# The end of a decoder trunk: the last expert weights requested before the wait for the scatters, the weighting of results behind the last pair's low parts, and all four token sums on TensorE

## The chip, the cores and the metric

The kernel runs on one core of one Trainium2 chip. The metric is the device time of one execution in microseconds, lower is better; the median of three runs before the change is 745.61 us.

Four engines appear below: TensorE (PE, matmuls; PEld are its weight loads), VectorE (DVE), ScalarE (ACT) and GpSimd (POOL). SyncE (SP) issues most DMA transfers from its own instruction queue (SPq). Each engine runs its own instructions in program order; semaphores order work between engines.

## The reference

One layer of `x + mixers(norm(x))`, then `x + moe(norm(x))`, then a final RMSNorm, for 512 tokens of width 1024 in float32. The change sits in the last two steps:

```
t = xn.reshape(b * s, d)                      # 512 x 1024
# each token picks one group of 8 experts, and 2 experts in it; combine holds their two weights
for e in range(32):
    hid = silu(t @ w_expert_gate[e]) * (t @ w_expert_up[e])      # width 256
    out = out + combine[:, e:e + 1] * (hid @ w_expert_down[e])
x = x + out
return rms_norm(x, final_norm_g)
```

## The kernel before, in words

The mixers come first and are not touched. The MoE then runs in 17 turns: 16 pairs of experts, and one turn between them for tokens that overflow an expert. An expert has 64 slots for tokens, so a pair fills the 128 partitions. In each turn TensorE multiplies the gathered tokens by the pair's gate and up weights (L1911, 64 matmuls), transposes the next pair's tokens (L1884), transposes the hidden rows (L1929), and multiplies by the down weights in two column halves `b` (L1950, 8 matmuls each); `y_ps` counts these halves. ScalarE and VectorE move the two halves out of PSUM into `ye`, and GpSimd scatters the rows to `y_dram` in HBM. The weights, 1 MB for each of the three matrices of an expert, arrive in a ring of 20 slots (`raw_slots`, named `ring_z`, `ring_x`, `ring_y`, `ring_w`, `ring_h`, `ring_p`, `ring_e`), requested by SyncE in order of use; `wait_reuse` (L477 ff.) holds each request until its slot is free.

The last two pairs (`KEPT`, turns 15 and 16) are not scattered. Their outputs are weighted on chip and split in a high part `yeh` (ScalarE, L976) and a low part `yel` (VectorE, the `stt` helper L1013), 128x512 for each half. `kept_products(k, t)` (L1868) adds them to the token sums of tile `t` by a one-hot matrix `pick`: two halves, each a `yeh` and a `yel` matmul of 512 columns. `k` is 0 for turn 15 and 1 for turn 16. All other results are read back from `y_dram` into four token tiles `yt[0]` to `yt[3]` (buffers `ring_z`, `ring_x`, `ring_x`, `ring_y`), two requests of 512 KB per tile, both counted by one semaphore. `gather_results` (VectorE) then forms x2 + w0 y0 + w1 y1 per tile in two operations on 128x1024; `comb_in` counts them.

The end, which the change touches:

- SyncE (L543 to L552) waits for the last two scatters, requests the results, and only then the two down matrices of the last pair, as four half-matrices: the first column halves with `d_half`, then the second ones.
- VectorE in the last turn weights tile 0 ahead of `hid`, tiles 1 and 2 ahead of the first low part, tile 3 between the low parts.
- The PSUM sums `TOTALS` are two banks per tile. Down products go to banks 5 and 6, the transposed hidden rows to bank 4. TensorE adds the weighted results of tiles 0 and 1 into their sums by `add_sum` (L1876), two float32 matmuls with the identity; tiles 2 and 3 are added by VectorE instead (`added`, L1533), two operations of 128x512 each. TensorE finishes the tiles in the order 3, 0, 2, 1, and they are normed and stored in the order 0, 3, 1, 2.
- For each tile ScalarE squares and sums a row (L1003) and takes the root (L1005); VectorE takes the reciprocal (L1524) and scales by it and `final_norm_g` (`scaled`, one 128x1024 `stt`); SyncE stores it (L570).
- Before the norms, every engine reads `flag`, a number in SBUF, and branches on it. With these inputs the branch is not taken.

## Times and profile before

| | us |
|---|---|
| three runs | 744.25, 745.61, 746.86 |
| median | 745.61 |
| span of the profiled execution, first to last instruction | 742.8 |
| median less span | 2.8 |
| PE, PEld, DVE, ACT, POOL busy | 696.6, 512.4, 342.6, 245.7, 90.3 |

The profile gives one execution by its span alone; the 2.8 us between it and the median stand for what lies around the span (the runs themselves lie 2.61 us apart). The trace gives each instruction its start and duration in us from the span's start, and behind it, in brackets, how long its engine was idle before it and what ended that. A row can merge several instructions (x8). In the rows, a matmul's duration contains the drain of its pipeline, so consecutive matmuls overlap.

### The profile page before, as it was taken

How to read it: one execution, taken by the hardware profiler on the slowest of the kernel's cores; microseconds unless marked ns; L12 is line 12 of the kernel's file. 1: busy time of each engine (PE TensorE's matmuls, PEld its weight loads, DVE VectorE, ACT ScalarE, POOL GpSimd, SP SyncE). 2: the span in 40 equal slices, each digit the busy share in tenths (PEclk: the TensorE clock that was granted, in tenths of full speed). 3: DMA queues.
4: the chain of work that ended last, by engine and by line, in shares of the span. 5: the costliest groups of instructions: out<-in, count | busy, mean ns of one | idle time of the engine just before them, and what ended most of it. 6: DMA issues, size and time to landing. Idle time of an engine off the chain costs nothing.

```text
span 742.8 us, 9617 instructions
## 1 busy us (share of the span) xinstructions
PE 696.6 (94%) x3863; PEld 512.4 (69%) x3863; DVE 342.6 (46%) x635; ACT 245.7 (33%) x397; POOL 90.3 (12%) x135
## 2 busy tenths in 40 slices
PE   5999999999999999999999999699999999978785
PEld 4888988877777777688888888566555564645443
DVE  5378994255556666555446215614211112112156
ACT  7232135465656666454243211200111111001014
POOL 2001912001010100200002000202111111211000
PEclk9999999999999999999999999789999999999998
DMA  6523234332221112392405699489999999999982
GB/s 230 170 67 105 93 87 142 128 127 72 71 67 41 59 48 70 104 336 71 138 5 226 277 367 345 164 324 394 415 420 421 419 422 420 417 421 418 423 330 116
DMA packets 61582, 166.58 MB, mean 224 GB/s; under 512 B 8084, under 2 KB 39905, under 8 KB 49116
## 3 DMA queue, kind: packets, MB, share of 16 engines
q1 hardware_dynamic: 55900, 153.86, 54.0%
q0 software_dynamic: 5632, 12.05, 4.3%
q8 instruction: 32, 0.52, 0.3%
q14 instruction: 18, 0.15, 0.1%
HBM read 158.31 MB, written 15.99 MB: 235 GB/s over the span
## 4 chain that ended last, share of the span: by engine, by line
PE 83%; DMA 8%; DVE 3%; ACT 2%; SPq 2%; issue 1%; POOL 0%; POOLq 0%; ACTq 0%; DVEq 0%
PE psum L1552 30%; PE psum L1911 12%; PE psum L1648 12%; PE psum L1950 7%; PE psum L1823 6%; DMA ring_y<-in_w_expert_up 4%; PE psum L1660 3%; DMA ring_e<-in_w_expert_down 2%; PE psum L1700 2%; PE psum L1727 1%; DMA y_dram<-ye,slots 1%; PE psum L1673 1%; PE psum L1929 1%; PE psum L1716 1%; SPq L552 1%
## 5 line engine op out<-in xcount | busy, mean ns | idle before, releaser
L1552 PE MATMUL psum<-xh,wh 128*128 128x512 f32 x256 | 99.9, 390 | 1.5 <-DVE xl L1013 1.5
L1552 PE MATMUL psum<-xh,wl 128*128 128x512 f32 x256 | 99.7, 389 | 0.0
L1552 PE MATMUL psum<-xl,wh 128*128 128x512 f32 x256 | 99.6, 389 | 0.0
L1016 DVE TENSOR_TENSOR wl<-raw,wh 128x1280 fp32r<-128x1280 f32 (+4 forms) x37 | 71.8, 1946 | 40.8 <-ACT wh L761 21.2
L1013 DVE SCALAR_TENSOR_TENSOR hid<-psum,rslot,act_g 128x256 f32<-128x256 f32 x17 | 8.2, 484 | 119.8 <-ACT act_g L967 119.8
L967 ACT ACTIVATE act_g<-psum,rslot 128x256 f32<-128x256 f32 x17 | 8.0, 473 | 155.4 <-PE psum L1911 155.4
L1552 PEld LDWEIGHTS psum<-xh,wh 128*128 128x128 f32 x256 | 48.1, 188 | 11.5 <-DVE xl L1013 1.7
L1552 PEld LDWEIGHTS psum<-xh,wl 128*128 128x128 f32 x256 | 48.1, 188 | 10.1
L1552 PEld LDWEIGHTS psum<-xl,wh 128*128 128x128 f32 x256 | 48.1, 188 | 9.9
L1648 PE MATMUL psum<-xh,wh 128*128 128x512 f32 x128 | 53.1, 415 | 0.0
L1648 PE MATMUL psum<-xh,wl 128*128 128x512 f32 x128 | 50.2, 392 | 0.0
L1648 PE MATMUL psum<-xl,wh 128*128 128x512 f32 x128 | 50.0, 390 | 0.0
L1013 DVE SCALAR_TENSOR_TENSOR sg<-cu,ch,sg 128x512 f32<-128x512 f32 x60 | 48.8, 884 | 0.0
L1911 PE MATMUL psum<-ring_w,xT 128*64 128x256 f32 x224 | 40.2, 394 | 4.9 <-DMA ring_h<-in_w_expert_up 4.9
L1911 PE MATMUL psum<-ring_h,xT 128*64 128x256 f32 x224 | 38.8, 384 | 1.3 <-DMA ring_e<-in_w_expert_up 1.3
L1468 DVE COPY ye<-psum 128x512 f32<-128x512 f32 x15 | 10.4, 692 | 59.4 <-PE psum L1950 59.4
L667 POOL DMA_INDIRECT y_dram<-ye,slots x15 | 15.2, 1010 | 172.8 <-DVE ye L1468 160.2
L1911 PE MATMUL psum<-ring_e,xT 128*64 128x256 f32 x208 | 34.8, 394 | 0.0
L1911 PEld LDWEIGHTS psum<-ring_w,xT 128*64 128x64 f32 x224 | 23.3, 142 | 12.7 <-issue 7.2
L1911 PEld LDWEIGHTS psum<-ring_h,xT 128*64 128x64 f32 x224 | 23.0, 139 | 11.7 <-issue 3.9
L1222 DVE TENSOR_TENSOR gp<-gs,psum 128x512 f32<-128x512 f32 x16 | 11.0, 687 | 39.2 <-PE psum L1552 38.4
L894 ACT ACTIVATE gs<-psum,bg 128x512 f32<-128x512 f32 x16 | 10.9, 687 | 52.6 <-PE psum L1552 52.6
(329 smaller groups left out, 1495.2 us busy)
## 6 DMA issues: line engine op xcount, KB each, us to landing
raw<-in_w_gate SPq DMA_DIRECT2D x16, 1024.0 KB, 6.2
raw<-in_w_in SPq DMA_DIRECT2D x9, 1024.0 KB, 5.8
ring_w<-in_w_expert_gate SPq DMA_DIRECT2D x7, 1024.0 KB, 22.9
ring_w<-in_w_expert_up SPq DMA_DIRECT2D x7, 1024.0 KB, 21.8
ring_h<-in_w_expert_gate SPq DMA_DIRECT2D x7, 1024.0 KB, 22.7
ring_h<-in_w_expert_up SPq DMA_DIRECT2D x7, 1024.0 KB, 24.6
ring_e<-in_w_expert_up SPq DMA_DIRECT2D x7, 1024.0 KB, 28.9
ring_h<-in_w_expert_down SPq DMA_DIRECT2D x6, 1024.0 KB, 25.1
```

The costliest lines, as they stand in the source:

```text
L667: pool.indirect_dma_start(out=y_dram[:, :], out_offset=bass.IndirectOffsetOnAxis(ap=slots[n, p], axis=0), in_=ye[n, s, :], in_offset=None, ...
L894: act.activation(gs[:, m, :], gate_bank(cg, m)[:, :], ACT.Sigmoid, bias=bg[:, d:d + 1]).then_inc(S["gate_mul"], 1)
L1013: return dve.scalar_tensor_tensor(out=out_, in0=a, scalar=s, in1=b, op0=o0, op1=o1)
L1016: return dve.tensor_tensor(dst, src, hi.bitcast(F32), ALU.subtract)
L1222: dve.tensor_tensor(gp[:, m, :], gs[:, m, :], branch_bank(cg, m)[:, :], ALU.mult).then_inc(S["gate_free"], 1)
L1552: last = nc.tensor.matmul(dst, a, b, start=start and n == 0, stop=stop and n == len(seq) - 1)
L1648: last = nc.tensor.matmul(bank[6 + n % 2][:, :], a[:, c, f], b[:, c, :], start=c == 0 and q == 0, stop=c == KC - 1 and q == 2)
L1660: last = nc.tensor.matmul(bank[5][:, :], a[:, j, f], b[g][:, j, :], start=j == 0 and q == 0, stop=j == BJ - 1 and q == 2)
L1700: nc.tensor.matmul(bank[0][:, q0:], k_s[r:r + HD, j, kt * P:(kt + 1) * P], q_s[r:r + HD, j, q0:], start=True, stop=True).then_inc(S["z_psu ...
L1823: last = nc.tensor.matmul(bank[t][:, :], x_[:, t, c, :], w_[:, b, c, :], start=c == 0 and m == 0, stop=c == KC - 1 and m == 2)
L1911: last = nc.tensor.matmul(bank[2][half, m * FE:(m + 1) * FE], xT[:, k, half], w[h][:, k, :], start=k == 0 and m == 0, stop=k == KC - 1, sk ...
L1950: last = nc.tensor.matmul(bank[5 + b][half, :], hidT[:, m, half], w_d[h][:, m, b * T:(b + 1) * T], start=m == 0, stop=m == FE // P - 1)
```

## The change

Order of requests on SyncE: the last pair's two down matrices are requested whole, like all others, ahead of the wait for the scatters; the four half-matrix requests behind the results are gone, and with them the semaphore `d_half`. TensorE waits once, for both whole matrices.

VectorE: nothing of the results is weighted ahead of `hid`. Tile 0 is weighted ahead of both low parts, tiles 1 to 3 behind them.

Sums: `TOTALS[t]` is now banks 2t and 2t+1 for every tile; down products go to banks 4 and 5, the transposed hidden rows to bank 6. TensorE adds the weighted results of all four tiles; VectorE's `added` is gone. Tiles are finished, normed and stored in the order 0, 1, 2, 3.

```diff
-        TOTALS = [psum[:, 0:2, :], psum[:, 2:4, :], psum[:, 5:7, :], psum[:, 4:8:3, :]]
-        ADDED = NT // 2
-        SUMMED, NORMED = (3, 0, 2, 1), (0, 3, 1, 2)
+        TOTALS = [psum[:, 2 * t:2 * t + 2, :] for t in range(NT)]
...
-            last_down = [unit_no(0, LAST, half, 2) for half in range(2)]
-            for w in range(NU, last_down[0]):
+            for w in range(NU, len(units_of(0))):
...
             for s in range(2):
                 sp_e.wait_ge(scattered[s], 16 * (NPAIR // 2 - s))
             load_results()
-            for w in last_down:
-                wait_reuse(0, w)
-            for b in range(2):
-                for w in last_down:
-                    slot = ring_at(0, w)[0]
-                    i, kind, e = units_of(0)[w]
-                    cols = slice(b * T, (b + 1) * T)
-                    sp_e.dma_start(raw_slots[slot].rearrange("p (m n) -> p m n", m=FE // P)[:, :, cols],
-                                   ed_v[e].rearrange("p (m n) -> p m n", m=FE // P)[:, :, cols]).then_inc(ring_full[slot] if b else S["d_half"], 16)
...
-            for n, t in enumerate(NORMED):
-                sp_e.wait_ge(S["fin_last"], n + 1)
+            for t in range(NT):
+                sp_e.wait_ge(S["fin_last"], t + 1)
...
-            for n, t in enumerate(NORMED):
-                if t < ADDED:
-                    act.wait_ge(S["c_ps"], SUMMED.index(t) + 1)
-                    total = TOTALS[t]
-                else:
-                    act.wait_ge(S["comb"], NT - t)
-                    total = halves(yt[t][:, 0, :])
-                act.activation(halves(yt[t][:, 1, :]), total, ACT.Square, accum_out=stat[:, 0, t:t + 1]).then_inc(S["sq_done"], 1)
+            for t in range(NT):
+                act.wait_ge(S["c_ps"], t + 1)
+                act.activation(halves(yt[t][:, 1, :]), TOTALS[t], ACT.Square, accum_out=stat[:, 0, t:t + 1]).then_inc(S["sq_done"], 1)
...
-                    if isinstance(c, int) and i == LAST:
-                        gather_results(1, range(1))
                     dve.wait_ge(S["silu"], E + 1)
...
+                        if k:
+                            gather_results(1, range(1))
                         for b in range(2):
-                            if k:
-                                gather_results(1, range(1 + 2 * b, 3 + b))
                             half = slice(b * T, (b + 1) * T)
                             dve.wait_ge(S["y_hi"], 2 * k + b + 1)
-                            stt(yel[:, 1 - k, half], bank[5 + b][:, :], w_kept[:, k:k + 1], yeh[:, 1 - k, half].bitcast(F32),
+                            stt(yel[:, 1 - k, half], bank[4 + b][:, :], w_kept[:, k:k + 1], yeh[:, 1 - k, half].bitcast(F32),
                                 ALU.mult, ALU.subtract).then_inc(S["y_lo"], 1)
                         dve.sem_inc(S["y_b"], 1)
+                        if k:
+                            gather_results(1, range(1, NT))
...
             dve.wait_ge(S["gfin_in"], 16)
-            def scaled(t):
-
-                dve.wait_ge(S["root"], NT + 2 + NORMED.index(t))
+            for t in range(NT):
+                dve.wait_ge(S["root"], NT + 2 + t)
                 st.link(dve.reciprocal(stat[:, 2, t:t + 1], stat[:, 1, t:t + 1]))
-                total = TOTALS[t] if t < ADDED else halves(yt[t][:, 0, :])
-                stt(halves(yt[t][:, 0, :]), total, stat[:, 2, t:t + 1], halves(gfin[:, :]), ALU.mult, ALU.mult).then_inc(S["fin_last"], 1)
-
-            def added(t):
-
-                dve.wait_ge(S["c_ps"], SUMMED.index(t) + 1)
-                for b in range(2):
-                    half = slice(b * T, (b + 1) * T)
-                    ins = dve.tensor_tensor(yt[t][:, 0, half], yt[t][:, 0, half], TOTALS[t][:, b, :], ALU.add)
-                ins.then_inc(S["comb"], 1)
-
-            added(3)
-            scaled(0)
-            scaled(3)
-            added(2)
-            scaled(1)
-            scaled(2)
+                stt(halves(yt[t][:, 0, :]), TOTALS[t], stat[:, 2, t:t + 1], halves(gfin[:, :]), ALU.mult, ALU.mult).then_inc(S["fin_last"], 1)
...
             add_sum(0, 0, False)
-            for t in SUMMED:
-                if t == 1:
-                    add_sum(t, 0, False)
-                if t == 2:
-                    kept_products(0, t, True, False)
-                kept_products(1, t, False, True).then_inc(S["c_ps"], 1)
+            kept_products(1, 0, False, True).then_inc(S["c_ps"], 1)
+            kept_products(0, 2, True, False)
+            for t in range(1, NT):
+                kept_products(1, t, False, False)
+            for t in range(1, NT):
+                add_sum(t, 0, False).then_inc(S["c_ps"], 1)
```

SyncE's queue, from the last gate and up matrices to the results, before:

```order
L457 DMA ring_p1<-in_w_expert_gate 128x2048 [waits gu_done]
L457 DMA ring_e0<-in_w_expert_up 128x2048 [waits gu_done]
L540 DMA ring_z<-y_dram 128x1024 [waits sc1,sc0]
L540 DMA ring_z<-y_dram 128x1024
L540 DMA ring_x<-y_dram 128x1024 x4
L540 DMA ring_y<-y_dram 128x1024 x2
L552 DMA ring_e0<-in_w_expert_down 128x2x512 [waits gu_done]
```

and after the change (`sc0`, `sc1` are the scatters' semaphores):

```order
L455 DMA ring_p1<-in_w_expert_gate 128x2048 [waits gu_done]
L455 DMA ring_e0<-in_w_expert_up 128x2048 [waits gu_done]
L455 DMA ring_e0<-in_w_expert_down 128x2048 [waits gu_done]
L455 DMA ring_e1<-in_w_expert_down 128x2048 [waits gu_done]
L537 DMA ring_z<-y_dram 128x1024 [waits sc1,sc0]
L537 DMA ring_z<-y_dram 128x1024
L537 DMA ring_x<-y_dram 128x1024 x4
```

The down matrices moved from behind the eight requests for results to ahead of them, and ahead of the wait that these carry.

VectorE's last turn (`hid` is the hidden product, the `ring_` rows the weighting of results, `yel` the low parts), before:

```order
L1013 SCALAR_TENSOR_TENSOR ring_z<-ring_z,cw 128x1024 [waits comb_in]
L1013 SCALAR_TENSOR_TENSOR hid<-psum,rslot,act_g 128x256 [waits silu,comb_in]
L1013 SCALAR_TENSOR_TENSOR ring_x<-ring_x,cw,x2 128x1024 [waits x1]
L1013 SCALAR_TENSOR_TENSOR ring_x<-ring_x,cw 128x1024 [waits comb_in]
L1013 SCALAR_TENSOR_TENSOR ring_x<-ring_x,cw,x2 128x1024 [waits x2s,comb_in]
L1013 SCALAR_TENSOR_TENSOR ring_x<-ring_x,cw 128x1024 [waits comb_in]
L1013 SCALAR_TENSOR_TENSOR yel<-psum,w_kept,yeh 128x512 [waits y_hi,comb_in]
L1013 SCALAR_TENSOR_TENSOR ring_y<-ring_y,cw,x2 128x1024 [waits x3]
L1013 SCALAR_TENSOR_TENSOR ring_y<-ring_y,cw 128x1024 [waits comb_in]
L1013 SCALAR_TENSOR_TENSOR yel<-psum,w_kept,yeh 128x512 [waits y_hi,comb_in]
L1474 TENSOR_LOAD flag [waits flag_ready]
```

and after the change:

```order
L996 SCALAR_TENSOR_TENSOR hid<-psum,rslot,act_g 128x256 [waits silu]
L996 SCALAR_TENSOR_TENSOR ring_z<-ring_z,cw,x2 128x1024 [waits x0]
L996 SCALAR_TENSOR_TENSOR ring_z<-ring_z,cw 128x1024 [waits comb_in]
L996 SCALAR_TENSOR_TENSOR yel<-psum,w_kept,yeh 128x512 [waits y_hi,comb_in]
L996 SCALAR_TENSOR_TENSOR yel<-psum,w_kept,yeh 128x512 [waits y_hi]
L996 SCALAR_TENSOR_TENSOR ring_x<-ring_x,cw,x2 128x1024 [waits x1]
L996 SCALAR_TENSOR_TENSOR ring_x<-ring_x,cw 128x1024 [waits comb_in]
L996 SCALAR_TENSOR_TENSOR ring_x<-ring_x,cw,x2 128x1024 [waits x2s,comb_in]
L996 SCALAR_TENSOR_TENSOR ring_x<-ring_x,cw 128x1024 [waits comb_in]
L996 SCALAR_TENSOR_TENSOR ring_y<-ring_y,cw,x2 128x1024 [waits x3,comb_in]
L996 SCALAR_TENSOR_TENSOR ring_y<-ring_y,cw 128x1024 [waits comb_in]
L1457 TENSOR_LOAD flag [waits flag_ready,comb_in]
```

Six weighting operations moved from ahead of a low part to behind both, and the load of `flag` has gained a wait for the last of them.

TensorE's last instructions ahead of its own load of `flag` (`pick0` and `pick1` are the one-hot matrices of turns 15 and 16), before:

```order
L1868 MATMUL psum<-yeh,pick1 128x512
L1868 MATMUL psum<-yel,pick1 128x512
L1868 MATMUL psum<-yeh,pick1 128x512
L1868 MATMUL psum<-yel,pick1 128x512
L1876 MATMUL psum<-ring_x,ident 128x512 x2
L1868 MATMUL psum<-yeh,pick1 128x512
L1868 MATMUL psum<-yel,pick1 128x512
L1868 MATMUL psum<-yeh,pick1 128x512
L1868 MATMUL psum<-yel,pick1 128x512
L1964 TENSOR_LOAD flag
```

and after the change:

```order
L1825 MATMUL psum<-yeh,pick1 128x512
L1825 MATMUL psum<-yel,pick1 128x512
L1825 MATMUL psum<-yeh,pick1 128x512
L1825 MATMUL psum<-yel,pick1 128x512
L1833 MATMUL psum<-ring_x,ident 128x512 x4
L1833 MATMUL psum<-ring_y,ident 128x512 x2
```

The identity products of tiles 1, 2 and 3 now end the sums; before, one of them stood ahead of the last group of four.

## Rows read from the trace of the kernel before

**Rows 1.** The page: its span, and the chain that ended last, by engine.

```profile
span 742.8 us, 9617 instructions
...
PE 83%; DMA 8%; DVE 3%; ACT 2%; SPq 2%; issue 1%; POOL 0%; POOLq 0%; ACTq 0%; DVEq 0%
```

**Rows 2.** The chain of waits, 680 to 743 us: start, duration, what.

```profile
711.46 13.35 DMA ring_e<-in_w_expert_down
...
728.79 3.90 PE psum L1868 x16
```

**Rows 3.** Timeline of SyncE's queue: start, duration of issue, request.

```profile
680.65 3.56 SPq L457 DMA_DIRECT2D ring_e<-in_w_expert_up  x1
700.23 0.81 SPq L540 DMA_DIRECT2D ring_z<-y_dram  x2
...
705.30 8.30 SPq L552 DMA_DIRECT2D ring_e<-in_w_expert_down  x4
...
738.37 1.72 SPq L570 DMA_DIRECT2D out<-ring_x  x2
```

**Rows 4.** Busy time by stretch; the last two columns are DMA share and GB/s.

```profile
680.00:700.00 20.00, 14.89 (x102) 9.44 (x100) 2.37 (x4) 1.45 (x3) 1.01 (x1) 0.91 1.01 418
```

**Rows 5.** Tiles ring_z and ring_y, 700 to 720 us: results' requests, time to landing.

```profile
DMA to landing us min/median/max: 7.7/9.6/11.4
...
DMA to landing us min/median/max: 12.6/14.4/16.2
```

**Rows 6.** Timeline of TensorE's matmuls: start, duration, instruction, idle before.

```profile
704.83 3.65 PE L1950 MATMUL psum<-ring_h,hidT 128*64 128x512 f32 x16 [0.47 <-ACT hidT L969]
...
709.81 0.40 PE L1911 MATMUL psum<-ring_h,xT 128*64 128x256 f32 x1 [1.33 <-DMA ring_e<-in_w_expert_up]
...
720.11 0.39 PE L1868 MATMUL psum<-yel,pick 128*128 128x512 f32 x1
722.29 1.94 PE L1950 MATMUL psum<-ring_e,hidT 128*64 128x512 f32 x8 [1.78 <-DMA ring_e<-in_w_expert_down]
724.94 1.94 PE L1950 MATMUL psum<-ring_e,hidT 128*64 128x512 f32 x8 [0.72 <-DMA ring_e<-in_w_expert_down]
...
732.53 1.88 PE L1876 MATMUL psum<-ring_x,ident 128*128 128x512 f32 x4
```

**Rows 7.** Timeline of VectorE, 707 to 743 us.

```profile
707.59 0.75 DVE L1013 SCALAR_TENSOR_TENSOR yel<-psum,w_kept,yeh 128x512 fp32r<-128x512 f32 x1 [2.60 <-ACT yeh L976]
709.25 0.75 DVE L1013 SCALAR_TENSOR_TENSOR yel<-psum,w_kept,yeh 128x512 fp32r<-128x512 f32 x1 [0.90 <-ACT yeh L976]
...
717.61 0.48 DVE L1013 SCALAR_TENSOR_TENSOR hid<-psum,rslot,act_g 128x256 f32<-128x256 f32 x1 [2.95 <-ACT act_g L967]
...
719.33 1.28 DVE L1013 SCALAR_TENSOR_TENSOR ring_x<-ring_x,cw 128x1024 f32<-128x1024 f32 x1
720.65 1.28 DVE L1013 SCALAR_TENSOR_TENSOR ring_x<-ring_x,cw,x 128x1024 f32<-128x1024 f32 x1
...
728.42 0.75 DVE L1013 SCALAR_TENSOR_TENSOR yel<-psum,w_kept,yeh 128x512 fp32r<-128x512 f32 x1
730.11 1.28 DVE L1533 TENSOR_TENSOR ring_y<-ring_y,psum 128x512 f32<-128x512 f32 x2 [0.94 <-PE psum L1868]
...
736.85 0.17 DVE L1524 RECIPROCAL stat<-stat 128x1 f32<-128x1 f32 x1 [0.40 <-ACT stat L1005]
737.05 1.28 DVE L1013 SCALAR_TENSOR_TENSOR ring_x<-psum,stat,gfin 128x1024 f32<-128x1024 f32 x1
...
738.44 1.28 DVE L1013 SCALAR_TENSOR_TENSOR ring_x<-ring_x,stat,gfin 128x1024 f32<-128x1024 f32 x1
```

**Rows 8.** Timeline of ScalarE, 728 to 736 us.

```profile
728.21 1.28 ACT L995 ACT_TABLE_LOAD   x1 [0.60 <-issue]
...
735.38 1.02 ACT L1003 ACTIVATE ring_x<-psum 128x1024 f32<-128x1024 f32 x1 [1.66 <-PE psum L1868]
```

**Rows 9.** Tensor out: the four stores, time from issue to landing.

```profile
DMA to landing us min/median/max: 2.6/3.0/4.4
```

More of the change, by code:

```diff
@@ L1478, in _ @@
                 for t in range(NT):
-                    if t < ADDED:
-                        ins = dve.tensor_copy(halves(x2[:, t, :]), TOTALS[t])
-                    else:
-                        for b in range(2):
-                            half = slice(b * T, (b + 1) * T)
-                            ins = dve.tensor_tensor(x2[:, t, half], yt[t][:, 0, half], TOTALS[t][:, b, :], ALU.add)
-                    ins.then_inc(S["rank_ready"], 1)
+                    dve.tensor_copy(halves(x2[:, t, :]), TOTALS[t]).then_inc(S["rank_ready"], 1)
                 n = NT
@@ L1515, in _ @@
                 dve.wait_ge(S["c_ps"], 2 * NT)
-                for t in range(ADDED, NT):
-                    dve.memset(yt[t][:, 0, :], 0.0).then_inc(S["rank_ready"], 1)
-                dve.wait_ge(S["rank_ready"], PASSES - 1 + n + (NT - ADDED))
             dve.wait_ge(S["gfin_in"], 16)
-            def scaled(t):
-                dve.wait_ge(S["root"], NT + 2 + NORMED.index(t))
+            for t in range(NT):
+                dve.wait_ge(S["root"], NT + 2 + t)
                 st.link(dve.reciprocal(stat[:, 2, t:t + 1], stat[:, 1, t:t + 1]))
-                total = TOTALS[t] if t < ADDED else halves(yt[t][:, 0, :])
-                stt(halves(yt[t][:, 0, :]), total, stat[:, 2, t:t + 1], halves(gfin[:, :]), ALU.mult, ALU.mult).then_inc(S["fin_last"], 1)
-            def added(t):
-                dve.wait_ge(S["c_ps"], SUMMED.index(t) + 1)
-                for b in range(2):
-                    half = slice(b * T, (b + 1) * T)
-                    ins = dve.tensor_tensor(yt[t][:, 0, half], yt[t][:, 0, half], TOTALS[t][:, b, :], ALU.add)
-                ins.then_inc(S["comb"], 1)
-            added(3)
-            scaled(0)
-            scaled(3)
-            added(2)
-            scaled(1)
-            scaled(2)
+                stt(halves(yt[t][:, 0, :]), TOTALS[t], stat[:, 2, t:t + 1], halves(gfin[:, :]), ALU.mult, ALU.mult).then_inc(S["fin_last"], 1)
         @block.tensor
@@ L1875, in add_sum @@
                 for b in range(2):
-                    last = nc.tensor.matmul(TOTALS[t][:, b, :], ident[:, :], yt[t][:, 0, b * T:(b + 1) * T], start=start, stop=start,
+                    last = nc.tensor.matmul(TOTALS[t][:, b, :], ident[:, :], yt[t][:, 0, b * T:(b + 1) * T], start=start, stop=True,
                                             skip_group_check=True)
@@ L1928, in expert_pass @@
                     for m in range(FE // P):
-                        last = nc.tensor.transpose(bank[4][:, m * P:(m + 1) * P], hid[:, :].rearrange("p (n m) -> p m n", m=FE // P)[:, m, :], ident[:, :])
+                        last = nc.tensor.transpose(bank[6][:, m * P:(m + 1) * P], hid[:, :].rearrange("p (n m) -> p m n", m=FE // P)[:, m, :], ident[:, :])
                     last.then_inc(S["ht_ps"], 1)
@@ L1938, in expert_pass @@
                         kept_products(0, 3, True, False)
-                        pe.wait_ge(S["d_half"], 32)
-                        w_d = [raw_slots[ring_at(c, unit_no(c, i, h, 2))[0]].rearrange("p (m n) -> p m n", m=FE // P) for h in halves]
-                    else:
-                        w_d = [loaded(h, 2).rearrange("p (m n) -> p m n", m=FE // P) for h in halves]
+                    w_d = [loaded(h, 2).rearrange("p (m n) -> p m n", m=FE // P) for h in halves]
                     for b in range(2):
-                        if b and isinstance(c, int) and i == LAST:
-                            for h in halves:
-                                loaded(h, 2)
                         for m in range(FE // P):
@@ L1949, in expert_pass @@
                                 half = slice(h * SLOT, (h + 1) * SLOT)
-                                last = nc.tensor.matmul(bank[5 + b][half, :], hidT[:, m, half], w_d[h][:, m, b * T:(b + 1) * T],
+                                last = nc.tensor.matmul(bank[4 + b][half, :], hidT[:, m, half], w_d[h][:, m, b * T:(b + 1) * T],
                                                         start=m == 0, stop=m == FE // P - 1)
```

14 lines of the change are left out of this document (7 added, 7 removed).

## The prediction, made before the changed kernel was run

> **What bounds the kernel now.** I read the page first: the span is 742.8 us and the chain that ended last is 83% TensorE and 8% DMA [rows 1]. The change leaves everything up to turn 16 as it is, so only the end matters. The chain of waits there passes through the down weights of the last pair, requested at 711.46 and landed 13.35 us later, at 724.81 [rows 2]. TensorE's timeline shows what that costs: it has issued all it can by 720.34 (the last pass starts at 720.11, the pitch below is 0.23), stands 1.78 us before the first half of the down products and 0.72 us before the second [rows 6]. That is the wait the change removes: 2.50 us, 0.34% of the time.
>
> SyncE's timeline shows why the weights are late. Its last gate or up request is issued at 680.65 to 684.21; then it is silent until the scatters are in at 700.23, requests results, and only from 705.30 the down weights [rows 3]. The transfers never paused meanwhile, 418 GB/s from 680 to 700 [rows 4]. A backlog is being drained in order, so the place in the queue decides a landing, and the request time does not.
>
> **Part 1, the down weights first.** The two requests are 2.10 MB, at 418 GB/s 5.0 us. Turn 16's gate and up weights have landed at 709.8 [rows 6]; the down weights stand right behind them and land at 709.8 + 5.0 = 714.8. Needed at 720.34: a margin of 5.5 us. The same 5.0 us push the results back. Tile 0's second request goes out at about 700.6 and is in by 11.4 us later, 712.0; tile 3's last one at about 703.5 is in 16.2 us later, 719.7 [rows 3, 5]. Now: tile 0 at 717.0, tiles 1, 2, 3 each 2.55 us later, the last at 724.7. The bytes and the draining are the same, so the gate and up landing stays where it is; SyncE issues the two requests in the 16 us in which it stood still, and the eight results still go out at 700.23.
>
> The first request for results seems to land after 7.7 us, at 707.9, ahead of weights requested 19 us before it [rows 5, 6], which would speak against draining in order. The Trainium skill, "DMA: Bandwidth & Descriptors", section "Why a DMA increments its semaphore by 16 and not by 1", says that a transfer is spread over 16 engines that finish independently and that two transfers on one semaphore can fill each other's count. By that rule 7.7 us is no landing of tile 0's first half, only the 11.4 us is one, and the order per engine holds; read the other way, the results would share the rate with what is ahead of them, which is the second rival below.
>
> **Part 2, the down products start at 720.34.** Turn 15 gives the rhythm without a wait: down products from 704.83, first low part at 707.59 (+2.76), second at 709.25 (+4.42) [rows 6, 7]. So in turn 16: low parts at 723.10 and 724.76, the second over at 725.5. Before, it was over at 729.17 [rows 7]. Gained at this point: 3.7 us, 2.5 from the waits and the rest because tile 3's weighting no longer stands between the low parts. Tile 0's weighting starts behind `hid`, at about 718.1, with 717.0 as its landing, and is over by 720.8, in time for 723.10.
>
> **Part 3, the weighting moves behind the low parts.** Six operations at a pitch of 1.32 us (719.33 to 720.65 [rows 7]) start at about 725.5 (pipelined, as 728.42 follows its forerunner at once): tile 1 is done at 728.1, tile 2 at 730.7, tile 3 at 725.5 + 5 x 1.32 + 1.28 = 733.4. Their landings (719.6, 722.1, 724.7) are all earlier, so no wait there. Four of these six had been hidden in the wait for the weights; now all stand on VectorE's path.
>
> **Part 4, sums on TensorE.** A group of four `kept_products` passes costs 0.92 us (16 passes 3.90 us with a drain of 0.16 [rows 2]). An `add_sum` costs: from 732.53 to the end of the group behind it, 735.35, are 2.82 us, less 0.92 and the drain 0.16: 1.74 us [rows 6, 8]. TensorE: down products 3.65 us with overlap 0.07, to 723.9; `add_sum(0)` to 725.7, after the low part's end at 725.5; five groups 4.6 to 730.3; three `add_sum` 5.2 to 735.5 (tile 3's weighting, at 733.4, is before its turn at 733.8); drain 0.16, so 735.7. The two extra `add_sum` cost TensorE 3.5 us and free VectorE of 2 x 1.28 = 2.6 us [rows 7]. From the last sum to the end of the last scaling: before, 735.38 [rows 8] to 738.33 (737.05 + 1.28 [rows 7]), 2.95 us. TensorE's path would end at 738.6, against 739.72 (738.44 + 1.28) before: -1.1 us.
>
> **Part 5, VectorE's path, which ends last.** Behind the last weighting stand the load of `flag`, the branch, and four scalings. Scalings that wait for nothing have a pitch of 1.39 us (737.05 to 738.44), and the reciprocal leads by 0.20 us (736.85 to 737.05) [rows 7]. The roots are there: tile 0's sum is ready at about 726.8, tile 1's at 732.2, tile 2's at 733.9, and tile 3's root at 735.7 + 1.47 = 737.2 (735.38 to 736.85). So the end is 733.4 + g + 0.20 + 3 x 1.39 + 1.28 = 739.05 + g, where g is the gap for `flag` and branch. The trace does not show it alone. ScalarE's is 0.60 us of plain issue [rows 8]. VectorE's own gap is 0.94 us at most, since it ends with a wait for TensorE [rows 7]. Before, the load could start while the low part ran: from 728.42 to 730.11 are 1.69 us, an upper end; now it carries a wait for the last weighting, so nothing of it hides. From below: 0, if it hides after all. I take 0.95, next to VectorE's own row. Ends: 739.1 to 740.7; taken 740.0, +0.3 us.
>
> The Trainium skill, "DMA: Bandwidth & Descriptors", section "Latency and other measured facts", gives a floor of about 600 ns for a `tensor_load`; if that is this load, ScalarE's 0.60 agrees, and by it alone the end would be 739.65, -0.1 us.
>
> **Part 6, the stores.** Before, the last store is issued at 739.75 and the span ends 3.08 us after the last scaling [rows 1, 3, 7]. The four landed after 2.6 to 4.4 us [rows 9]. Now all four come 1.39 us apart, and 512 KB take 1.25 us at 418 GB/s, so they just fit; the last may meet its forerunner. Between 0 and 4.4 - 2.6 = 1.8 us; I take 0.1, since the last two of before also came 1.38 us apart.
>
> **Sum.** -1.1 us if TensorE's path ended last; VectorE's does: +0.3, stores +0.1, so +0.4 us on the span: 743.2, with the 2.8 us around it 746.0. The gain of 3.7 us at the low parts is paid back on VectorE: from the end of the second low part to its last scaling were 10.55 us before (729.17 to 739.72) and are 14.5 now, 7.9 more for the six weightings, 2.6 less for the additions, and the rest in waits for sums and roots that fall away. No change is my forecast. What a measurement of this kernel can tell from no change is about 0.3%, 2.2 us.
>
> **The rivals.**
>
> *The removed wait is worth its full size.* If the gap g hides and the weighting runs into TensorE's slack, the end is TensorE's 738.6: 744.5, still within 0.3%. To pass below 743.4 the removed waits would also have to be longer in the timed runs than in the profiled one; by 1.3 us, half of the 2.6 us by which the runs lie apart, it is 743.2. For: 4 MB sit ahead of those weights, and any delay among them is added to the wait. Against: VectorE's 14.5 us behind the low parts, which no early weights shorten. Chance 6%.
>
> *Results late in front of the low parts.* Tile 0's weighting is now ahead of both low parts, and VectorE waits for its landing with the low parts, TensorE's groups and everything else behind it. It decides from a landing after 720.5 (723.10 less two operations), one us for one. If the results shared the rate instead of draining in order, all eight would land near 724.7: low parts at 727.4, 4.3 us later, end 750.3. It passes 0.3% from 722.3 on. For it: the 7.7 us above. Against: the landings 2.55 us apart, in the order of the requests. Chance 7%.
>
> *Stores and flag at their upper ends.* g of 1.69 and 1.8 us for the stores give +2.8 us, 748.4. For: one store of four did take 4.4 us. Against: the last two did not. Chance 7%.
>
> *The change doesn't do what it says*: the weights don't come before 720.34, since SyncE's issue was itself slow, 3.56 us for one request [rows 3]. Landing at 722.2, as the first half now, moves everything 1.9 us: 747.9. Against: 16 us for two requests. Chance 3%.
>
> **How the numbers follow.** Forecast, no change at 746.0: 77%; the rivals 6, 7, 7 and 3%. Within 0.3% fall the forecast and 3 of the last two rivals' 10, which lie close to the bound of 747.8: 80%. Slower: late results 7 and the other 7 of those 10, 14%. Faster: 6%. The range takes 744.0 (TensorE's path, and 0.5 of spread) to 748.1 (the rivals of the stores and the late weights), leaving out the late results and most of the faster case.
>
> **What would show it.** Down weights requested from about 684 and landed by 716; down products from 720.3 without a break of 3.65 us; low parts at 723.1 and 724.8; six weighting operations in a row from 725.5 to 733.4; a gap of 0.6 to 1.7 us on VectorE, then four scalings 1.39 us apart with no wait for a root; TensorE done by 735.7; last scaling over at 740.0. Wrong: a DMA wait ahead of tile 0's weighting, a wait on `comb_in` of over 0.5 us on TensorE, or scalings that wait for roots.

## The result, and the profile of the changed kernel

| | before | changed |
|---|---|---|
| median of the timed runs | 745.25 us (742.11 to 746.86, 12 runs) | 747.50 us (744.56 to 749.76, 12 runs) |
| ratio, changed to before | | 1.0031, 95% interval 1.0016 to 1.0045 |
| span of the profiled execution | 742.8 us | 747.0 us |
| last scaling over, to the end of the span | 3.08 us | 4.53 us |

The forecast was no change at 746.0. The time lies in the range (744.0 to 748.1), but 0.31% is not nothing: the interval lies wholly above 1 and across my bound of 0.3%. A small slowdown is the honest reading, and it is what the third rival, flag and stores at their upper ends, had described.

The spans lie 4.2 us apart, more than the medians. SyncE's queue shows a part of why:

```profile
682.62 3.13 SPq L455 DMA_DIRECT2D ring_e<-in_w_expert_up  x1
685.80 4.70 SPq L455 DMA_DIRECT2D ring_e<-in_w_expert_down  x2
...
738.33 0.34 SPq L558 DMA_DIRECT2D out<-ring_z  x1
739.72 1.72 SPq L558 DMA_DIRECT2D out<-ring_x  x2
742.50 0.33 SPq L558 DMA_DIRECT2D out<-ring_y  x1
```

The last up request goes out at 682.62, against 680.65 before [rows 3], and it stands ahead of the first request that the change moves (685.80). So 1.9 of the 4.2 us arose before the change acts; runs of one kernel lie further apart than that, and two later profiles with the changed kernel's requests have their first product at 709.64 and 709.38 (e2 and e9 below). From here on I measure every kernel from one event, the first gate/up product of turn 16 (711.70 here, 709.81 before [rows 6]). Call the time from there to the end of the span R. It is 35.30 us, against 32.99: 2.31 us more. 0.86 us of it stand before the last scaling is over (30.77 against 29.91), 1.45 behind it.

The chain of waits from that product on (start, duration, what) has lost the DMA piece of rows 2 and gained a row of VectorE's:

```profile
722.32 3.61 PE psum L1901 x16
...
726.67 0.03 DVE yel L996
...
733.94 1.30 DVE ring_y L996
735.23 0.03 issue
735.26 0.54 DVEq L1457
...
736.15 0.07 DVEq L1458
736.22 0.53 issue
```

The removed wait did go: TensorE's down products (L1901) run 3.6 us without a break behind its last pass, where it stood 1.78 and 0.72 us before [rows 6]. From 726.67 VectorE carries the chain to the end. L1457 is its load of `flag`, L1458 the branch: 735.26 to 736.15 for the one, and 0.07 with 0.53 of issue behind it for the other. VectorE's timeline answers to rows 7:

```profile
721.14 1.28 DVE L996 SCALAR_TENSOR_TENSOR ring_z<-ring_z,cw 128x1024 f32<-128x1024 f32 x1
725.09 0.75 DVE L996 SCALAR_TENSOR_TENSOR yel<-psum,w_kept,yeh 128x512 fp32r<-128x512 f32 x1 [2.66 <-ACT yeh L964]
726.67 0.75 DVE L996 SCALAR_TENSOR_TENSOR yel<-psum,w_kept,yeh 128x512 fp32r<-128x512 f32 x1 [0.84 <-ACT yeh L964]
727.34 1.28 DVE L996 SCALAR_TENSOR_TENSOR ring_x<-ring_x,cw,x 128x1024 f32<-128x1024 f32 x1
...
733.94 1.28 DVE L996 SCALAR_TENSOR_TENSOR ring_y<-ring_y,cw 128x1024 f32<-128x1024 f32 x1
736.82 0.16 DVE L1497 RECIPROCAL stat<-stat 128x1 f32<-128x1 f32 x1 [1.60 <-issue]
737.02 1.28 DVE L996 SCALAR_TENSOR_TENSOR ring_z<-psum,stat,gfin 128x1024 f32<-128x1024 f32 x1
...
741.19 1.28 DVE L996 SCALAR_TENSOR_TENSOR ring_y<-psum,stat,gfin 128x1024 f32<-128x1024 f32 x1
```

Low parts, six weightings in a row, a hole of 1.60 us, four scalings at the rhythm of 1.39 us: from 726.67 on VectorE stands still only in that hole. TensorE is done sooner, its last sum being ready 3.7 us before that tile's scaling starts:

```profile
732.21 3.59 PE L1833 MATMUL psum<-ring_x,ident 128*128 128x512 f32 x8
735.64 1.88 PE L1833 MATMUL psum<-ring_y,ident 128*128 128x512 f32 x4
```

Busy time by stretch, last two columns DMA share and GB/s, shows the end of the stores:

```profile
742.00:743.00 1.00, 0.00 (x0) 0.00 (x0) 0.47 (x1) 0.00 (x0) 0.00 (x0) 0.95 1.00 397
743.00:744.00 1.00, 0.00 (x0) 0.00 (x0) 0.00 (x0) 0.00 (x0) 0.00 (x0) 0.50 0.92 365
744.00:745.00 1.00, 0.00 (x0) 0.00 (x0) 0.00 (x0) 0.00 (x0) 0.00 (x0) 0.50 0.65 262
745.00:746.00 1.00, 0.00 (x0) 0.00 (x0) 0.00 (x0) 0.00 (x0) 0.00 (x0) 0.50 0.06 25
746.00:747.00 1.00, 0.00 (x0) 0.00 (x0) 0.00 (x0) 0.00 (x0) 0.00 (x0) 0.50 0.01 4
```

The bulk is out by 745; in the two microseconds after it 25 and then 4 GB/s move, 6% and 1% of the 16 DMA engines. 6% is one engine of 16: one has fallen behind. The four stores (tile `out`) land after

```profile
DMA to landing us min/median/max: 2.7/3.9/4.1
```

where before it was 2.6, 3.0 and 4.4 [rows 9]. The slowest is not slower, but it is now the last one. In the same view of before, the lag is there too, and is worked off in the pause of 3.1 us ahead of its third store, issued at 738.37:

```profile
736.00:737.00 1.00, 0.00 (x0) 0.00 (x0) 0.60 (x2) 0.97 (x4) 0.00 (x0) 1.00 0.92 361
737.00:738.00 1.00, 0.00 (x0) 0.00 (x0) 0.96 (x2) 0.97 (x3) 0.00 (x0) 1.00 0.41 160
738.00:739.00 1.00, 0.00 (x0) 0.00 (x0) 0.96 (x3) 0.19 (x1) 0.00 (x0) 0.92 0.07 25
739.00:740.00 1.00, 0.00 (x0) 0.00 (x0) 0.73 (x1) 0.00 (x0) 0.00 (x0) 0.50 0.83 336
```

The trace also shows what was in the way. Besides the packets of the stores, one packet of 16 KB moves in the burst, from a queue that the trace marks `instruction`. In the changed kernel from 740 to 742.5 us (queue, kind: packets, MB, share of the 16 engines' time):

```profile
q1 hardware_dynamic: 245, 0.88, 88.5%
q8 instruction: 1, 0.02, 3.6%
```

3.6% of 16 times 2.5 us is 1.4 us of one engine: the packet starts at 740.64 and takes 1.45 us, where a packet of the stores, 4 KB, mostly takes 0.16. The four stores landed after 2.7, 3.9, 3.8 and 4.1 us, and the second was under way at that moment. In before's trace such a packet, 0.92 us long, starts at 736.69 and meets the first pair of stores (3.4 and 4.4 us); from 738 on there is none (2.7 and 2.6 us).

### The profile page after: what moved, and what is told of

It is laid out like the page before. It is cut to its first block, busy times and chain, and to the rows that moved or that the text cites. A ratio compares the mean times of both kernels' runs of the same rounds, so it can differ in the third digit from the quotient of the medians.

```text
span 747.0 us, 9626 instructions
## 1 busy us (share of the span) xinstructions
PE 703.9 (94%) x3871; PEld 514.5 (69%) x3871; DVE 340.0 (46%) x631; ACT 245.8 (33%) x397; POOL 90.9 (12%) x135
## 4 chain that ended last, share of the span: by engine, by line
PE 81%; DMA 9%; DVE 4%; SPq 3%; ACT 2%; issue 1%; POOL 0%; DVEq 0%; ACTq 0%; POOLq 0%
PE psum L1509 29%; PE psum L1605 12%; PE psum L1868 12%; DMA ring_e<-in_w_expert_up 8%; PE psum L1780 6%; PE psum L1901 6%; PE psum L1617 3%; SPq L455 3%; PE psum L1657 2%; PE psum L1684 1%; PE psum L1630 1%; DVE ring_x L996 1%; PE psum L1673 1%; PE psum L1739 1%; PE psum L1517 1%
## 5 line engine op out<-in xcount | busy, mean ns | idle before, releaser
L1868 PEld LDWEIGHTS psum<-ring_e,xT 128*64 128x64 f32 x208 | 21.7, 146 | 9.9 <-issue 2.8
```

The lines of the kernel that those rows point to most:

```text
L1868: last = nc.tensor.matmul(bank[2][half, m * FE:(m + 1) * FE], xT[:, k, half], w[h][:, k, :], start=k == 0 and m == 0, stop=k == KC - 1, sk ...
```

## The experiments

R splits into "scaled" (first gate/up product of turn 16 to the end of the last scaling) and "tail" (from there to the end of the span); landings are the middle and the longest of the stores. All from one profiled execution each. The ratio is that of the timed runs to before's on the same chip, with its 95% interval; where none stands, the kernel was run once.

| kernel | first product | scaled | tail | R | landings | ratio |
|---|---|---|---|---|---|---|
| before | 709.81 | 29.91 | 3.08 | 32.99 | 3.0, 4.4 | |
| changed | 711.70 | 30.77 | 4.53 | 35.30 | 3.9, 4.1 | 1.0031 (1.0016 to 1.0045) |
| e1_flag_early | 710.43 | 29.88 | 4.69 | 34.57 | 3.5, 4.2 | 1.0020 (1.0001 to 1.0039) |
| e2_one_store | 709.64 | 30.77 | 3.09 | 33.86 | 2.6 | |
| e3_down_first | 709.68 | 30.16 | 3.06 | 33.22 | 2.7, 4.4 | 1.0008 (0.9989 to 1.0027) |
| e4_old_order | 708.95 | 33.69 | 3.06 | 36.75 | 2.6, 4.0 | |
| e5_down_and_order | 709.65 | 33.65 | 3.10 | 36.75 | 2.6, 2.6 | 1.0066 (1.0042 to 1.0089) |
| e6_two_ahead | 711.87 | 30.50 | 3.73 | 34.23 | 3.5, 4.2 | 1.0000 (0.9982 to 1.0019) |
| e7_two_ahead_flag | 711.64 | 28.80 | 3.66 | 32.46 | 3.5, 4.2 | 0.9993 (0.9974 to 1.0012) |
| e8_rebalanced | 709.22 | 28.51 | 3.37 | 31.88 | 3.1, 3.4 | 0.9995 (0.9975 to 1.0015) |
| e9_two_queues | 709.38 | 30.77 | 4.35 | 35.12 | 3.9, 3.9 | |
| e10_last_halved | 712.80 | 28.64 | 3.06 | 31.70 | 2.9, 3.2 | 0.9985 (0.9966 to 1.0004) |

Should an expectation number the parts of the change, 1 is the down weights first, 2 the weighting's place and 3 the sums by TensorE; my own text calls them by these names.

The theory: the hole for flag and branch, and the stores' tail, are what the change costs beyond the forecast; the rest of its sum holds.

### e1_flag_early: VectorE loads `flag` ahead of the low parts

```diff
                         if k:
                             gather_results(1, range(1))
+                            load_flag()      # waits for flag_ready, value_load
...
-            dve.wait_ge(S["flag_ready"], 1)
-            most = dve.value_load(flag[0:1, 0:1], min_val=0, max_val=T)
+            most = early[0]
             with dve.If(most > SLOT):
```

> The changed kernel, with VectorE's load of flag moved ahead of both low parts, into the 2.66 us in which VectorE waits there; the branch stays behind the last weighting. Measure: from the first gate/up product of turn 16 to the end of the span (35.3 us in the changed kernel, 33.0 before). Theory (the load sits in the gap of 1.60 us, 0.54 + 0.21 and what lies between, about 0.85, and VectorE's chain sets the end): the gap falls to 0.7 to 0.8 us and the stretch to 34.4 to 34.5. Rival (the gap is the branch and what follows it, the load costs nothing): the gap stays above 1.4 us, the stretch at 35.2 or more. Rival (TensorE's sums set the end): the gap falls, the scalings of tiles 0 to 2 come earlier, tile 3's waits for its root and the stretch stays within 0.2 us of 35.3.

The last scaling is over 0.89 us sooner after the first product than in the changed kernel. The chain shows that the loading is gone from the hole and the branch is not:

```profile
733.97 0.03 issue
734.00 0.07 DVEq L1465
734.07 0.53 issue
```

So of the 1.60 us, 0.89 are the load and 0.71 the branch. R is 34.57, just above the 34.4 to 34.5 that I had expected, since the tail did not shrink (4.69 against 4.53).

### e2_one_store: only the last tile is stored

Tiles 0 to 2 of the output are never written.

```diff
-            for t in range(NT):
-                sp_e.wait_ge(S["fin_last"], t + 1)
-                sp_e.dma_start(out_v[t], yt[t][:, 0, :]).then_inc(S["out_done"], 16)
+            sp_e.wait_ge(S["fin_last"], NT)
+            sp_e.dma_start(out_v[NT - 1], yt[NT - 1][:, 0, :]).then_inc(S["out_done"], 16)
```

> The changed kernel with the stores of tiles 0, 1 and 2 left out (their output is missing); only tile 3 is stored, after its scaling. Theory (the stores queue up behind one another: four of 512 KB 1.39 us apart): alone, the store lands 2.6 to 2.8 us after its issue instead of 4.1, and from the end of the last scaling to the end of the span are 3.1 us instead of 4.53. Rival (the long landing belongs to the last store itself, whatever is ahead of it): landing near 4.1, 4.5 us from the last scaling to the end.

"Scaled" is the changed kernel's to the hundredth, 30.77, and the tail drops from 4.53 to 3.09 us with a landing of 2.6. The three stores ahead of the last one are worth 1.44 us. The `instruction` packet comes here too, at 738.32, 28.7 us after the first product (28.9 in the changed kernel), but no store is under way then. So the burst is what carries a delay to the end.

### e3_down_first: before, with the down weights first and nothing else

```diff
-            for w in range(NU, last_down[0]):
+            for w in range(NU, len(units_of(0))):
...
-            for w in last_down:      # and the loop that requested them in halves
```

> The kernel before with the first part of the change alone: both down matrices of the last pair requested whole, ahead of the wait for the scatters; weighting order and sums as before. Theory (the results land 5 us later, and VectorE waits for tile 0 ahead of hid): hid starts 2 to 2.5 us later than before against the gate/up landing, TensorE waits there instead of at the down products, the second low part ends within 0.5 us of where it did, and the stretch from the first gate/up product of turn 16 to the end is 33.0 to 33.6 us (33.0 before). Rival (the removed wait is worth its 2.5 us by itself): 30.5 to 31.

The removed wait comes back in another place. VectorE, which still weights tile 0 ahead of `hid`, now waits for the results that the weights have pushed back:

```profile
716.88 1.28 DVE L1003 SCALAR_TENSOR_TENSOR ring_z<-ring_z,cw,x 128x1024 f32<-128x1024 f32 x1 [7.02 <-DMA ring_z<-y_dram]
718.20 1.28 DVE L1003 SCALAR_TENSOR_TENSOR ring_z<-ring_z,cw 128x1024 f32<-128x1024 f32 x1
719.52 0.48 DVE L1003 SCALAR_TENSOR_TENSOR hid<-psum,rslot,act_g 128x256 f32<-128x256 f32 x1
```

716.88 is 7.20 us behind the first product, and so is the landing of tile 0 that the prediction worked out (717.0, 7.2 behind 709.81). Counted from the first product, `hid` starts 2.0 us later than before (9.84 against 7.80 [rows 7]), and TensorE stands 2.14 us before the transpose of it. R is 33.22: with the weights alone moved, 2.5 us of removed wait change the end by +0.23 us, and the timed runs tell no difference.

### e4_old_order and e5_down_and_order: the parts in pairs

e4 is the changed kernel with the weighting in its old place; e5 has the down weights first and the weighting's new place, with the sums of two tiles still added by VectorE.

```diff
# e4, against the changed kernel
+                    if isinstance(c, int) and i == LAST:
+                        gather_results(1, range(1))
                     dve.wait_ge(S["silu"], E + 1)
...
                         for b in range(2):
+                            if k:
+                                gather_results(1, range(1 + 2 * b, 3 + b))
...
-                            gather_results(1, range(1, NT))
# e5, against e3: the order of the changed kernel
-                        gather_results(1, range(1))          # ahead of hid
...
+                            gather_results(1, range(1))      # ahead of the low parts
...
+                            gather_results(1, range(1, NT))  # behind them
```

> The changed kernel with its second part undone: tile 0 weighted ahead of hid, tiles 1 and 2 ahead of the first low part, tile 3 between them; down matrices first and all sums on TensorE stay. Theory: the second low part ends at about 19.5 us after the first gate/up product (15.7 in the changed kernel), TensorE's remaining 9 us of sums then set the end: stretch 35.1 to 36.5 us. Rival (the weighting behind the low parts was the mistake, the rest a gain): below 33.0.

> The kernel before with the first two parts of the change, down matrices first and the weighting behind the low parts; the sums of tiles 2 and 3 still added by VectorE. Theory (VectorE's path ends last and the two additions, 2.6 us, come on top of it): VectorE's last scaling ends about 2 to 2.6 us later than in the changed kernel against the gate/up landing, the stretch is 37 to 38 us, so moving the sums to TensorE was worth its cost. Rival (TensorE's sums set the end in the changed kernel): with 3.5 us less work on TensorE the stretch falls below 35.3.

Both end 36.75 us after the first product, 3.8 later than before; for e5 I had expected 37 to 38. In e5 the additions stand on the path that is already the longest:

```profile
734.78 1.29 DVE L1523 TENSOR_TENSOR ring_y<-ring_y,psum 128x512 f32<-128x512 f32 x2 [1.60 <-issue]
...
739.01 1.28 DVE L1523 TENSOR_TENSOR ring_x<-ring_x,psum 128x512 f32<-128x512 f32 x2
```

The two additions with their gaps cost 2.88 us against the changed kernel. In e4 it is TensorE: `hid` is held up as in e3, and all sums follow, so that VectorE waits for roots, for the second of them 3.80 us:

```profile
732.44 0.16 DVE L1497 RECIPROCAL stat<-stat 128x1 f32<-128x1 f32 x1 [2.37 <-ACT stat L988]
...
737.73 0.16 DVE L1497 RECIPROCAL stat<-stat 128x1 f32<-128x1 f32 x1 [3.80 <-ACT stat L988]
```

It ended later than I had expected (35.1 to 36.5), and its granted clock was low behind the standstill of 2.15 us ahead of the transpose (columns: PE, PEld, DVE, ACT, POOL busy, clock, DMA share, GB/s):

```profile
720.00:722.00 2.00, 2.00 (x7) 1.56 (x6) 1.93 (x3) 0.28 (x1) 0.00 (x0) 0.57 0.27 111
722.00:724.00 2.00, 2.00 (x6) 0.54 (x7) 1.96 (x2) 0.00 (x0) 0.00 (x0) 0.57 0.04 14
724.00:726.00 2.00, 2.00 (x12) 0.70 (x10) 0.45 (x1) 0.69 (x1) 0.00 (x0) 1.00 0.00 0
```

e3 stood as long at the same place, 2.14 us, and kept its full clock:

```profile
720.00:722.00 2.00, 1.94 (x9) 1.66 (x10) 1.96 (x3) 0.39 (x1) 0.00 (x0) 1.00 0.36 145
```

The two kernels' `hid` starts 9.86 and 9.84 us after the first product, and the second low part 20.37 and 18.82: the low clock cost e4 1.55 us. Without it, by my estimate, e4's R would be 35.2, within what I had expected.

So the weighting's place and the sums need each other. On top of e3 the new place alone (e5) costs 3.5 us (33.65 scaled, against 30.16), and the sums alone (e4) cost 3.5 us as profiled and about 2.0 without the loss of clock; both together cost 0.6 (30.77).

The two kernels also test the stores. e5's stores come 1.63 us and more apart and all land after 2.6 us. From 736 us to the end only their own packets move, no `instruction` packet:

```profile
q1 hardware_dynamic: 576, 2.10, 49.6%
```

e4's first store is issued 5.3 us ahead of the next, alone, and lands after 4.0 us. An `instruction` packet of 1.20 us starts at 734.91, while it is under way. The issue, the landing and that packet (733.9 to 736.5 us):

```profile
733.95 0.34 SPq L558 DMA_DIRECT2D out<-ring_z  x1
...
DMA to landing us min/median/max: 4.0/4.0/4.0
...
q8 instruction: 1, 0.02, 2.9%
```

So a store needs no neighbour to be late. The three behind it land after 2.6 us.

### e6_two_ahead and e7_two_ahead_flag: shorten VectorE's path

e6 weights tile 1, too, ahead of the low parts, in the 2.66 us that VectorE waits there; e7 adds the load of `flag` ahead of `hid`.

```diff
-                            gather_results(1, range(1))
+                            gather_results(1, range(2))
...
-                            gather_results(1, range(1, NT))
+                            gather_results(1, range(2, NT))
```

> The changed kernel, with tile 1 weighted ahead of the low parts too, in the 2.66 us in which VectorE waits there. Measure as before: first gate/up product of turn 16 to the end of the span (changed kernel 35.3, before 33.0). Theory (VectorE's path sets the end, and TensorE's sums stand 2 us behind it): the last weighting ends 2.6 us earlier, then TensorE's sum of tile 3 sets the end; the last scaling ends 1.9 to 2.0 us earlier, stores 1.7 us apart do not queue and save 1.4 us more: 31.9 to 32.1; with the stores still queueing 33.3. Rival (tile 1's results land after 722.5 on the changed kernel's clock and hold up the low parts): the first low part starts later than 13.5 us after the first gate/up product and the gain shrinks by as much.

> As the kernel with tile 1 ahead of the low parts, and the load of flag moved ahead of hid, where VectorE waits over 6 us. Theory (TensorE's sums set the end once tile 1 is out of the way): the gap behind the last weighting falls by 0.9 us, tile 0's scaling comes earlier, but the last scaling ends within 0.2 us of where it does with tile 1 ahead alone; stretch 31.9 to 33.3 like that kernel's. Rival (VectorE's path still sets the end): 0.8 to 0.9 us shorter than that kernel.

e7 ends its scalings 28.80 after the first product, 1.97 sooner than the changed kernel, and they now wait for roots, which shows TensorE's path as the next bound:

```profile
735.53 0.16 DVE L1505 RECIPROCAL stat<-stat 128x1 f32<-128x1 f32 x1 [0.82 <-ACT stat L988]
...
737.25 0.16 DVE L1505 RECIPROCAL stat<-stat 128x1 f32<-128x1 f32 x1 [0.24 <-ACT stat L988]
```

That is the 1.1 us below before that I had worked out for TensorE's path (28.80 against 29.91). The profile of e6 is a miss by its own numbers, for another reason. TensorE stood 3.06 us before turn 16, and the first products came at half clock (columns: PE busy, granted clock, DMA share, GB/s):

```profile
710.00:712.00 2.00, 0.13 (x2) 1.00 1.03 428
712.00:714.00 2.00, 2.00 (x12) 0.50 0.99 410
714.00:716.00 2.00, 2.00 (x16) 0.65 1.02 420
```

0.50 is 1.2 GHz of 2.4. The down products came 12.24 us after the first product instead of 10.55, 1.69 us; without it "scaled" would be 28.81, within 0.01 of e7's, as expected of the two. Whether the timed runs carry this loss, their interval can't tell.

I had also expected that stores 1.7 us apart do not queue. That was wrong: e7's stores, issued 1.7 us apart behind the first, land after 2.9, 4.2, 3.7 and 3.2 us, with an `instruction` packet of 1.28 us at 737.90, and the tails are 3.66 and 3.73 us. The spacing sets how fast a delay is made up, about 0.5 us per store here and next to nothing at 1.39 us (3.9, 3.8 and 4.1 in the changed kernel).

### e8_rebalanced: what the experiments point to

The requests for tiles 0 and 1 go ahead of the down weights and those of 2 and 3 behind; `flag` and tile 0 stand ahead of `hid`, tile 1 ahead of the low parts; TensorE adds tiles 0 to 2, VectorE tile 3.

```diff
-            for w in range(NU, len(units_of(0))):
+            for w in range(NU, len(units_of(0)) - 2):
...
-            load_results()
+            load_results(range(2))
+            for w in range(len(units_of(0)) - 2, len(units_of(0))):
+                wait_reuse(0, w)
+                load_unit_no(w)
+            load_results(range(2, NT))
...
+                    if isinstance(c, int) and i == LAST:
+                        load_flag()
+                        gather_results(1, range(1))
```

> A version from the findings: results of tiles 0 and 1 requested ahead of the two whole down matrices, those of tiles 2 and 3 behind them; VectorE loads flag and weights tile 0 ahead of hid, tile 1 ahead of the low parts, tiles 2 and 3 behind; TensorE adds tiles 0, 1 and 2 (0 and 1 at once behind the down products), VectorE adds tile 3. Theory: down matrices land by 10.0 us after the first gate/up product, in time for 10.6; last weighting ends at 21.1, the last scaling at 28.6 us after it (29.9 before, 30.8 in the changed kernel), stretch 31.7 us, 33.1 if the stores queue; against the kernel before a ratio of 0.998 to 1.000. Rival (down matrices land late behind two tiles of results): TensorE waits for them, the stretch is above 32.5 by that wait.

"Scaled" came to 28.51 and R to 31.88, within 0.2 us of what was expected and 1.1 us below before. The timed runs cannot tell it from before.

### e9_two_queues: stores of tiles 1 and 3 from ScalarE's queue

```diff
-            for t in range(NT):
+            for t in range(0, NT, 2):          # SyncE
...
+            for t in range(1, NT, 2):          # ScalarE
+                act.wait_ge(S["fin_last"], t + 1)
+                act.dma_start(out_v[t], yt[t][:, 0, :]).then_inc(S["out_done"], 16)
```

> The changed kernel with the stores of tiles 1 and 3 issued from ScalarE's queue, those of tiles 0 and 2 from SyncE's. Theory (it is one of the 16 DMA engines that falls behind in the burst of four 512 KB stores, whichever queue they come from): the last store still lands some 3.9 to 4.1 us after its issue, last scaling to end of span 4.3 to 4.6 us, first gate/up product of turn 16 to end 35.1 to 35.4 (changed kernel: 4.1, 4.53, 35.30). Rival (SyncE's queue is what holds the stores up): the last lands in 2.6 to 2.8, 3.1 us after the last scaling, 33.8 to 34.0 in all.

Tail 4.35, R 35.12, and the last three stores land after 3.8 to 3.9 us. A second queue leaves the lag nearly as it was, so SyncE's queue is not what holds the stores up. The `instruction` packet is there as well, 1.40 us long at 738.21.

### e10_last_halved: e8 with the last tile scaled and stored in halves

```diff
+            for b in range(2):
+                half = slice(b * T, (b + 1) * T)
+                sp_e.wait_ge(S["fin_last"], NT + b)
+                sp_e.dma_start(out_v[NORMED[-1]][:, half], yt[NORMED[-1]][:, 0, half]).then_inc(S["out_done"], 16)
```

> e8_rebalanced with the last tile's scaling and store cut into two halves of its columns, 256 KB each. Theory (the last transfer is the shorter for being half as large and the lag of the trailing DMA engine is about the same): last store lands in 2.2 to 2.7 us (e8: 3.4), last scaling ends 0.05 to 0.1 later, last scaling to end 2.7 to 2.9 (3.37), first gate/up product of turn 16 to end 31.2 to 31.5 (31.88); ratio to before 0.997 to 0.999. Rival (a landing has a fixed price, and the lag of the trailing engine grows with each request): landing 3.0 or more, 31.8 or more in all, ratio as e8's 0.9995.

Tail 3.06 and R 31.70, between what the two theories expected. The list of DMA issues has the halves (KB each, median us from issue to landing):

```profile
out<-ring_x SPq DMA_DIRECT2D x2, 256.0 KB, 2.6
```

That is no sooner than a lone store twice the size. But the halves stand 0.7 us apart behind three other stores, so it isn't the price of 256 KB alone. Of the tail 0.3 us went, and 0.13 came back in the scaling. Its ratio, 0.9985 (0.9966 to 1.0004), is the best of all and still not told from before.

## Why the prediction was near, and where its sum failed

Each step in its own terms, all of them counted from the first gate/up product of turn 16.

- **Part 1** held. The weights were requested at 685.80 and never waited for. Tile 0's weighting started right behind `hid`, at 719.83, and was over at 722.42 (721.14 + 1.28), ahead of the low part at 725.09. The rival of late results fell.
- **Part 2** held. Down products began 10.55 us after the first product (forecast 10.53), low parts at 13.39 and 14.97 (13.29 and 14.95).
- **Part 3** held. Six weightings in a row, over at 23.52 (735.22), forecast 23.59. That the moved work would eat the whole gain was the point on which the sign hung; e3, e4 and e5 show it from the other side, since with one piece missing the removed wait buys nothing or costs.
- **Part 4** held. TensorE was done at 25.82 (735.64 + 1.88), forecast 25.89; e7, where VectorE's path is shorter, ends where I had put TensorE's.
- **Part 5, the gap g for flag and branch, is the first term mis-sized.** I took 0.95 between the ends 0 and 1.69; it was 1.60, 0.65 us more. I had written that nothing of it would hide any more, since the load now waits for the last weighting, and then took the value next to the row, VectorE's 0.94, in which some of it had still been hidden. The chain shows the load starting at 735.26, 0.04 behind the end of the last weighting: all of it in the open. The 0.60 us of ScalarE's row did not measure a load: ScalarE's own load starts at 727.00 and runs under its last activation (726.91 to 727.60), and what shows behind it is the branch, for which e1 gives 0.71 us on VectorE. The Trainium skill, "DMA: Bandwidth & Descriptors", section "Latency and other measured facts", puts the floor of a `tensor_load` at about 600 ns. That is two thirds of the 0.89 us that VectorE's load took, and nothing of the branch.
- **Part 6, the stores, is the second and larger.** I took 0.1 of a range up to 1.8; the tail grew by 1.45. I had argued from before's last two stores, 1.38 us apart and landed in 2.7 and 2.6, that a burst fits. But before's last pair came after a pause, and no `instruction` packet met it; one met the first pair, with its landing of 4.4, and that was the row that bore on four in a burst. The range named that row, and the sum ignored it.
- **The 2.8 us around the span** were wrong in kind: I added them as if the profiled execution were the median one. Each timed run comes with its span, and a run's time is its span and 2.1 us for before, 1.7 for the changed kernel. The profiled execution of before was thus near 745.0, and the changed kernel has 0.4 us less around its span.

Put together: +0.86 and +1.45, less 0.4, are +1.9 us, or 1.0026, in the measured interval. The forecast had +0.4; with the two missing terms, 0.65 and 1.35, and less the 0.4 around the span, it would have been +2.0.

What makes one DMA engine trail is not isolated by any run, but all twelve traces agree. Wherever a store landed after more than 2.8 us, an `instruction` packet of 16 KB moved while stores were under way, or just ahead of their data. In e2 and e5, where every landing is 2.6 us, none did. It explains what the spacing cannot: e4's lone store (4.0), e7's wide ones (4.2), and e8, which has the changed kernel's pitch of 1.39 us and a packet of 1.15 us right at the start of the burst: 3.4, 3.2, 3.0 and 2.9 us. In before the delay, 1.8 us, is twice the packet's own 0.92 us; packets of the stores that took 0.27 to 0.44 us just before and behind it make up the rest. The records don't name the engine of a packet, and no run moves this packet alone, so this stays an argument. What decides when the packet is due is open, and so is why the time around the span differs by 0.4 us between kernels.

## What to carry to other kernels

A wait that is taken away is worth no more than the slack of the next path: write down, engine by engine, what would end last if the wait were gone, and count there all that the edit moves, down to a load of one number and its branch. A late transfer counts only if nothing pauses behind it: price a burst of stores by the slowest of the stores before, not by the last, and look which other packets the DMA engines carry meanwhile. And compare kernels from an event that both share, not from the start of the span.

## What the runs showed of the hardware

- A load of one value and a branch on it cost VectorE 1.60 us when they stand behind its last operation: 0.89 for the load, 0.71 for the branch, which stays when the load is moved ahead (e1, e7).
- A store of 512 KB landed in 2.6 us when no `instruction` packet came near it (e2, e5). With one of 0.92 to 1.45 us in its way it took up to 4.4 (before, e3), alone too (4.0 in e4); in a burst 1.39 us apart the last store was still late (4.1 in the changed kernel), and 1.7 us apart each made up about 0.5 us (e7).
- After a standstill of 3.06 us the granted clock was 0.50 (1.2 GHz) for 2 us and 0.65 for 2 more, 1.69 us lost (e6); after one of 2.15 us it was 0.57 for 4 us (e4), and after one of 2.14 us at the same place it stayed 1.00 (e3); after 1.69 us, in the changed kernel, the first product ran at full speed (0.40 us).
- Issuing a request seems to take longer the more is queued ahead of it: two requests of 1 MB for down weights took 4.70 us at 685.80 in the changed kernel, and 0.94 us at 703.70 in e8.
